# Splitting the weights of attention's query, key and value in the slots of the weight ring

## The chip, the cores and the metric

The kernel runs on one core of a Trainium2 chip. The metric is the device time of one launch in microseconds (us). The kernel before takes 1962.6 us, the median of 3 runs (1962.38 to 1964.43).

## The reference, cut to what matters

One step of a two-layer encoder for 288 tokens (256 of a prompt and 32 of a sample) of width 1024. In each layer one projection feeds all branches of the token mixer:

```python
qa, ka, va, qi, ki, wi, qkv_b, a_b, b_b, z_b, gates = jnp.split(h @ w_in, SPLIT_POINTS, axis=-1)
o_a = dsa_attention(qa, qi, wi, k_all, v_all, ik_all, P)      # indexer scores, top-k keys, softmax over them
c, conv_new = causal_conv(qkv_b, conv_buf, conv_w)            # 1536 channels, then a gated delta rule
y = (g_a * (o_a @ w_oa) + g_b * (o_b @ w_ob)) @ w_out
```

`qa` (the attention's query) has 512 columns, `ka` and `va` (its key and value) 128 each, `qi` (the indexer's query) 512. The indexer computes `relu(qi . ik)`, weighs it by head, masks it and keeps the best keys of each token; the attention runs over these alone. Layer 0 ends in a dense feed-forward part, layer 1 in one of 8 experts, which is most of the span.

## The kernel before, in words

Everything lies transposed: the hidden state `hT` is 8 blocks of 128 channels by 288 tokens. A product of a 128-column weight block with it is one **output**: 8 contraction steps summed in one PSUM bank. A fp32 product is two matmul instructions. Other weights are **split**: ScalarE rounds the block to fp32r (the *high* part), VectorE subtracts it from the original (the *low* part), and three fp32r products (high by high, high by low, low by high) replace the fp32 one. The hidden state is split once a layer too (`hPh` by ScalarE, `hPl` by VectorE in 5 pieces, counted by `hpl_ready`).

**The ring.** All weights come through one ring of 6 slots of 1 MB (`RING`, `SLOT`, 2048 columns of fp32). A *unit* is what one slot holds; unit n lies in slot n modulo 6. SyncE loads the units in order (`load_units`, L339): unit n waits until the counter `unit_used` is at least n - 5, that is, until unit n - 6 has been released. TensorE releases a unit with the first ring matmul that follows its last reading (`rel.due`). An empty `unit()` reserves a slot and loads nothing: a pair of units holds one split block, of which the high part goes into the empty unit's slot and the low part over the weights themselves (`pair_slots`, L417; `ringr` is the same memory as `ring`, typed fp32r).

**The units of a layer**, in `project_units`: 0 small ones (indexer key, decay), 1 and 2 the indexer query, 3 and 4 the attention query (each 4 of 8 contraction blocks by 512 columns, 8 transfers of 128 KB), 5 key and value, and from 6 on 8 pairs for the conv channels and `z` (`pair_unit(l, j)` is 6 + 2j), then the gates.

**The stage around the change** is `front(l)`. Each engine has its own program, in an order written by hand, and waits on counters:

- TensorE: the small product; indexer queries 0 to 3 (`wide`); the decay sums; `indexer(0)`; `wide(P_QA)` (query 0); `indexer(1)`; query 1; `indexer_sample`; query 2; `score_sample`; query 3; key and value (`narrow`); conv 0 (`conv_product`, which uses pair j // 2 and waits for its low part by `pl_ready`); transposes; conv 1, 2, 3; `logits(0, 0)`; conv 4; `logits(0, 2)`; conv 5; and so on. Output m needs the bank of output m - 3 evicted (`room`).
- ScalarE: evictions, relus of the indexer's products, and the high parts of the pairs (`pair_high`, which waits for the weights and for the empty slot). In order: `relus(0)`, eviction of query 0, `relus(1)`, eviction of query 1, `relus_sample`, **`pair_high(0)`**, evictions of query 2, query 3 and key, `pair_high(1)`, eviction of the value, of conv 0, `news`, `pair_high(2)`.
- VectorE: small copies, the low parts of the hidden state, the decays (`g_ready`), a wait for `decay_done`, then `choose(0)`, **`pair_low(0)`**, a copy of the sample's score, `choose(1)`, `pair_low(1)`, `choose(2)`, `pair_low(2)`, and maxima, convolutions and further low parts in turn. `choose(i)` is the top-k of a block of tokens: 8 accumulations (L1430) and some 8 rounds of `max` and `match_replace` (L1438, L1439).
- GpSimd: masks, distances and slopes for the attention (`pen_ready`), then it waits for pair 1.

Of the kernel before, what the change touches and what calls it, by code (L numbers as in the profile page):

```python
# [19 lines left out]
P = 128  # L20
# [53 lines left out]
def program(nc, A, OUT, upto=99):  # L74
    ctx = ExitStack()
    with ctx:
# [169 lines left out]
        def project_units(l):  # L246
# [19 lines left out]
            assert (n0 + 1) % RING < RING - 1 and (n0 + 3) % RING < RING - 1  # L266
# [46 lines left out]
        N_PROJ, N_GATE, N_MERGE, N_FFN, N_EXP = 22, 16, 8, 3 * D_FF // 256, 3 * D_FFE // 256  # L313
# [98 lines left out]
        def pair_unit(l, j):  # L412
            return first["project", l] + 6 + 2 * j

        def pair_slots(l, j):

            n = pair_unit(l, j)  # L417
            return [ring[:, (n % RING) * SLOT:(n % RING) * SLOT + SLOT]] + [
                ringr[:, (x % RING) * SLOT:(x % RING) * SLOT + SLOT] for x in (n + 1, n)]

# [67 lines left out]
        const_ready, ln_turned = sem("const_ready"), sem("ln_turned")  # L488
        lnrow = arena[0:80, 0:P]
        with nc.Block() as block:  # L490
# [24 lines left out]
            def _(pe):  # L515
                pe.wait_ge(const_ready, 1)
                pe.wait_ge(ln_in, 160)
                nc.tensor.transpose(ps[0][:, 0:80], lnrow, ident[0:80, 0:80]).then_inc(ln_turned, 1)

            @block.vector  # L520
            def _(dve):
                dve.wait_ge(ln_turned, 1)
# [5 lines left out]
        masks_ready = sem("masks_ready")  # L528

        def masks(pool):  # L530
# [52 lines left out]
            nc.gpsimd.memset(std[:], 1.0).then_inc(masks_ready, 1)  # L583
# [5 lines left out]
        nrm_turned, out_stored = sem("nrm_turned"), sem("out_stored")  # L589

        def norm(call, j, g_vec=None, b_vec=None, final=False):

            gb = gb_all
            with nc.Block() as block:  # L594
# [15 lines left out]
                def _(dve):  # L610
# [25 lines left out]
                    for k in range(1, 0 if final else KD, 2):  # L636
                        dve.wait_ge(nrm_turned, k + 1)
# [5 lines left out]
                def _(act):  # L643
                    act.wait_ge(var_ready, call + 1)
                    nc.scalar.activation(std[:], rstd[:], ACT.Sqrt).then_inc(std_ready, 1)
                    for k in range(0, 0 if final else KD, 2):
                        act.wait_ge(nrm_turned, k + 1)
# [168 lines left out]
        def front(l):  # L816
# [25 lines left out]
            with nc.Block() as block:  # L842
# [22 lines left out]
                def _(pool):  # L865
# [17 lines left out]
                    nc.gpsimd.tensor_tensor(distr[:], distr[:].bitcast(F32), away[:].bitcast(F32), ALU.subtract).then_inc(pen_ready, 1)  # L883
                    pool.wait_ge(g_ready, l + 1)
# [7 lines left out]
                def _(pe):  # L892
                    def pairview(n):
                        s = (n % RING) * SLOT
                        return ring[:, s:s + 2 * SLOT].rearrange("p (k c) -> p k c", c=512)

# [4 lines left out]
                    def wide(m, n, c):  # L901

                        room(m)
                        w = pairview(n)
                        for k in range(KD):
                            if c == 0 and k % 4 == 0:
# [1909 lines left out]
```

## Time and profile before

| | |
|---|---|
| time, median of 3 runs | 1962.6 us |
| profiled execution | 1963.32 us, of which the span is 1961.5 us |
| TensorE (PE) busy | 1910.4 us |
| VectorE (DVE) busy | 1423.7 us |
| ScalarE (ACT) busy | 1134.7 us |
| GpSimd (POOL) busy | 90.0 us |
| mean granted TensorE clock | 0.991 of full speed |

A row of a timeline gives start and length in us, engine, source line, operation, what it writes and reads with shapes, and in brackets how long the engine sat idle before it and what ended that. Line 359 is the helper through which ring matmuls go; a matmul's length overlaps the next one's, so a group is timed from its start to the start of what follows. PEclk is the granted TensorE clock, 1.00 being 2.4 GHz.

### The profile page before, as it was taken

How to read it: one execution, taken by the hardware profiler on the slowest of the kernel's cores; microseconds unless marked ns; L12 is line 12 of the kernel's file. 1: busy time of each engine (PE TensorE's matmuls, PEld its weight loads, DVE VectorE, ACT ScalarE, POOL GpSimd, SP SyncE). 2: the span in 40 equal slices, each digit the busy share in tenths (PEclk: the TensorE clock that was granted, in tenths of full speed). 3: DMA queues.
4: the chain of work that ended last, by engine and by line, in shares of the span. 5: the costliest groups of instructions: out<-in, count | busy, mean ns of one | idle time of the engine just before them, and what ended most of it. 6: DMA issues, size and time to landing. Idle time of an engine off the chain costs nothing. (4 is left out here: it accounts for less than half of the span.)

```text
span 1961.5 us, 27193 instructions
## 1 busy us (share of the span) xinstructions
PE 1910.4 (97%) x11117; PEld 1649.6 (84%) x11117; DVE 1423.7 (73%) x1600; ACT 1134.7 (58%) x1256; POOL 90.0 (5%) x156
## 2 busy tenths in 40 slices
PE   6999999999999999999999999999999999999995
PEld 5889999999977889998888888888888888888884
DVE  4876265644338763575988979879799798897996
ACT  2465343544334663435776767767677677676773
POOL 5002000100031020001000000000000000000000
PEclk9999999999999999998999999999999999999998
DMA  6232174554421332462999999989999999999992
GB/s 170 86 94 93 44 199 134 172 169 156 153 77 45 93 114 65 104 230 65 372 357 318 370 327 350 370 300 373 344 334 368 318 358 357 317 373 331 343 369 106
DMA packets 260485, 456.98 MB, mean 233 GB/s; under 512 B 32218, under 2 KB 111274, under 8 KB 260356
## 3 DMA queue, kind: packets, MB, share of 16 engines
q1 hardware_dynamic: 258966, 454.74, 67.7%
q8 instruction: 91, 1.49, 0.3%
q10 hardware_dynamic: 1390, 0.44, 0.1%
q14 instruction: 38, 0.31, 0.0%
HBM read 452.11 MB, written 3.04 MB: 232 GB/s over the span
## 5 line engine op out<-in xcount | busy, mean ns | idle before, releaser
L390 DVE TENSOR_TENSOR wl<-ring,wh 128x2048 fp32r<-128x2048 f32 x385 | 880.5, 2289 | 245.3 <-ACT wh L384 242.1
L384 ACT ACTIVATE wh<-ring 128x2048 fp32r<-128x2048 f32 x385 | 739.6, 1923 | 318.0 <-PE ps L359 317.9
L359 PE MATMUL ps<-wh,xgh 128*128 128x512 f32 x896 | 354.3, 395 | 2.4 <-DVE wl L390 2.4
L359 PE MATMUL ps<-wh,xgl 128*128 128x512 f32 x896 | 349.3, 390 | 0.0
L359 PE MATMUL ps<-wl,xgh 128*128 128x512 f32 x896 | 349.1, 390 | 0.0
L359 PE MATMUL ps<-hPh,ringr 128*128 128x288 f32 x1024 | 229.3, 305 | 0.0
L359 PEld LDWEIGHTS ps<-wh,xgh 128*128 128x128 f32 x896 | 168.3, 188 | 40.0 <-DVE wl L390 5.7
L359 PEld LDWEIGHTS ps<-wh,xgl 128*128 128x128 f32 x896 | 168.2, 188 | 35.8
L359 PEld LDWEIGHTS ps<-wl,xgh 128*128 128x128 f32 x896 | 168.4, 188 | 33.2
L359 PEld LDWEIGHTS ps<-hPh,ringr 128*128 128x128 f32 x1024 | 170.6, 189 | 6.2 <-issue 2.5
L359 PE MATMUL ps<-hPl,ringr 128*128 128x288 f32 x512 | 152.0, 297 | 0.0
L359 PE MATMUL ps<-wh,gEh 128*128 128x512 f32 x448 | 143.4, 401 | 0.0
L359 PE MATMUL ps<-wl,gEh 128*128 128x512 f32 x448 | 139.6, 393 | 0.0
L359 PE MATMUL ps<-wh,gEl 128*128 128x512 f32 x448 | 138.1, 389 | 0.0
L359 PE MATMUL ps<-hTh,wh 128*128 128x288 f32 x352 | 103.3, 296 | 0.4 <-ACT hTh L711 0.4
L359 PE MATMUL ps<-hTh,wl 128*128 128x288 f32 x352 | 102.6, 294 | 0.0
L359 PEld LDWEIGHTS ps<-wh,gEl 128*128 128x128 f32 x448 | 84.1, 188 | 19.3
L359 PE MATMUL ps<-hTl,wh 128*128 128x288 f32 x352 | 99.6, 296 | 0.6 <-DVE hTl L2301 0.6
L359 PEld LDWEIGHTS ps<-wl,gEh 128*128 128x128 f32 x448 | 84.0, 188 | 18.9
L359 PEld LDWEIGHTS ps<-hPl,ringr 128*128 128x128 f32 x512 | 97.1, 190 | 0.1
L359 PE MATMUL ps<-hT,ring 128*128 128x288 f32 (+1 forms) x352 | 89.2, 410 | 1.9 <-PEq L594 0.9
L359 PEld LDWEIGHTS ps<-wh,gEh 128*128 128x128 f32 x448 | 78.9, 189 | 12.1
(415 smaller groups left out, 2792.2 us busy)
## 6 DMA issues: line engine op xcount, KB each, us to landing
ring<-in_moe_w SPq DMA_DIRECT2D x336, 1024.0 KB, 5.4
ring<-in_w_in SPq DMA_DIRECT2D x38, 1024.0 KB, 5.2
ring<-in_ffn_w SPq DMA_DIRECT2D x33, 1024.0 KB, 5.2
ring<-in_w_out SPq DMA_DIRECT2D x8, 1024.0 KB, 10.0
ring<-in_w_in SPq DMA_DIRECT2D x32, 128.0 KB, 3.2
ring<-in_w_oa SPq DMA_DIRECT2D x16, 256.0 KB, 5.3
ring<-in_w_ob SPq DMA_DIRECT2D x8, 512.0 KB, 7.2
resid<-in_x_prompt SPq DMA_DIRECT2D x1, 1024.0 KB, 5.2
```

The source lines that it names most:

```text
L359: ins = nc.tensor.matmul(*a, **k)
L384: nc.scalar.activation(wh[:, k % WS, :], ring[:, s:s + SLOT], ACT.Copy).then_inc(hi_ready, 1)
L390: ins = nc.vector.tensor_tensor(wl[:, k % WS, :], ring[:, s:s + SLOT], wh[:, k % WS, :].bitcast(F32), ALU.subtract)
```

## The change

The two query halves and the key/value block are split in ring slots like the conv pairs. Each of these three units is followed by an empty one, so a layer's projection has 25 units and not 22, and conv pair 0 is unit 9 of the layer. ScalarE makes the three high parts (`query_high`), VectorE the low parts of the two query halves, between `g_ready` and its wait for `decay_done`, and GpSimd the low part of key and value, behind `pen_ready`. The six outputs become three fp32r products a step (`query_product`, `query_terms`). The slots of a block are released by two: the first query half and its high part in the middle of query 3 (c == 3, k == 3), the second behind query 3, key/value behind the value. The rest of the orders stays. Besides, some counters are merged: `ln_turned` into `nrm_turned`, `masks_ready` into `const_ready`, `dl_in` into `st_in`.

```diff
@@ project_units
                 unit(*[(v[:, q, :, a, :], w[:, k + q, O_QA + 256 * a:O_QA + 256 * a + 256]
                         .rearrange("p (c x) -> p c x", x=HD)) for q in range(4) for a in range(2)])
+                unit()
             n = len(units)
             unit((slot(n, (8, 256)), w[:, :, O_KA:O_KA + 256]))
+            unit()
...
-        N_PROJ, N_GATE, N_MERGE, N_FFN, N_EXP = 22, 16, 8, 3 * D_FF // 256, 3 * D_FFE // 256
+        N_PROJ, N_GATE, N_MERGE, N_FFN, N_EXP = 25, 16, 8, 3 * D_FF // 256, 3 * D_FFE // 256
...
         def pair_unit(l, j):
-            return first["project", l] + 6 + 2 * j
+            return first["project", l] + 9 + 2 * j
...
+        def query_unit(l, j):
+            return first["project", l] + 3 + 2 * j
+
+        def query_high(act, l, j):
+
+            n = query_unit(l, j)
+            have(act, n)
+            if n + 2 > RING:
+                act.wait_ge(unit_used, n + 2 - RING)
+            w, h, _ = unit_pair(n)
+            nc.scalar.activation(h, w, ACT.Copy).then_inc(qa_high, 1)
+
+        def query_low(eng, engine, l, j, done):
+
+            eng.wait_ge(qa_high, 3 * l + j + 1)
+            w, h, r = unit_pair(query_unit(l, j))
+            engine.tensor_tensor(r, w, h.bitcast(F32), ALU.subtract).then_inc(done, 1)
...
@@ front, GpSimd
                     nc.gpsimd.tensor_tensor(distr[:], distr[:].bitcast(F32), away[:].bitcast(F32), ALU.subtract).then_inc(pen_ready, 1)
+                    query_low(pool, nc.gpsimd, l, 2, ka_low)
                     pool.wait_ge(g_ready, l + 1)
@@ front, TensorE
-                    def narrow(m, n, c):
+                    def query_product(m, c):
 
                         room(m)
                         if c == 0:
-                            have(pe, n)
-                        w = slot(n, (8, 256))
+                            pe.wait_ge(hpl_ready, 5 * (l + 1))
+                        if c == 4:
+                            pe.wait_ge(ka_low, l + 1)
                         for k in range(KD):
-                            ins = rel.mm(ps[m % 3][:, 0:T], w[:, k, P * c:P * c + P], hT[:, k, :], start=(k == 0), stop=(k == KD - 1))
+                            if c == 0 and k % 4 == 0:
+                                pe.wait_ge(qa_low, 2 * l + k // 4 + 1)
+                            for z, (x, y) in enumerate(query_terms(l, k, c)):
+                                ins = rel.mm(ps[m % 3][:, 0:T], x, y, start=(k == 0 and z == 0), stop=(k == KD - 1 and z == 2))
+                            if c == 3 and k == 3:
+                                rel.due, rel.slots = unit_used, 2
                         ins.then_inc(pj_done, 1)
-                        if c == 1:
-                            rel.due = unit_used
+                        if c in (3, 5):
+                            rel.due, rel.slots = unit_used, 2
...
-                    wide(P_QA, u0 + 3, 0)
+                    query_product(P_QA, 0)
                     indexer(1)
-                    wide(P_QA + 1, u0 + 3, 1)
+                    query_product(P_QA + 1, 1)
...
-                    narrow(P_KA, u0 + 5, 0)
-                    narrow(P_VA, u0 + 5, 1)
+                    query_product(P_KA, 4)
+                    query_product(P_VA, 5)
@@ front, ScalarE
                     nc.scalar.activation(hPh[:], hT[:], ACT.Copy).then_inc(hph_ready, 1)
+                    query_high(act, l, 0)
                     evac(P_QI + 1)
...
                     evac(P_QI + 2)
+                    query_high(act, l, 1)
                     evac(P_QI + 3)
                     relus(0)
+                    query_high(act, l, 2)
                     evac(P_QA)
@@ front, VectorE
                     nc.vector.tensor_copy(gvm[0:DEC, 2, 0:H4], gv[0:DEC, 2, :]).then_inc(g_ready, 1)
+                    query_low(dve, nc.vector, l, 0, qa_low)
+                    query_low(dve, nc.vector, l, 1, qa_low)
                     dve.wait_ge(decay_done, l + 1)
```

## Rows read from the trace of the kernel before

**Rows 1.** The page, busy time of each engine and its share of the span.

```profile
PE 1910.4 (97%) x11117; PEld 1649.6 (84%) x11117; DVE 1423.7 (73%) x1600; ACT 1134.7 (58%) x1256; POOL 90.0 (5%) x156
```

**Rows 2.** Busy time by stretch, layer 0: length; PE PEld DVE ACT POOL; clock; DMA.

```profile
47.00:74.50 27.50, 27.50 (x121) 20.03 (x120) 25.89 (x64) 10.11 (x21) 4.16 (x2) 1.00 0.25 77
...
91.30:163.00 71.70, 70.39 (x515) 62.28 (x514) 48.66 (x105) 42.05 (x98) 1.24 (x3) 1.00 0.31 96
```

**Rows 3.** Timeline of TensorE, layer 0: from query 0 to conv 4.

```profile
47.07 4.15 PE L359 MATMUL ps<-hT,ring 128*128 128x288 f32 x16
51.15 2.00 PE L964 MATMUL ps<-arena 64*128 64x256 f32 x16
...
57.15 0.76 PE L975 MATMUL ps<-arena 64*128 64x288 f32 x4
...
61.92 1.16 PE L982 MATMUL ps<-arena 128*32 128x288 f32 x4
63.01 11.91 PE L359 MATMUL ps<-hT,ring 128*128 128x288 f32 x48
...
91.31 0.30 PE L359 MATMUL ps<-hPh,ringr 128*128 128x288 f32 x1
...
94.61 0.70 PE L998 MATMUL ps<-arena 64*128 64x256 f32 x4
```

**Rows 4.** Timeline of VectorE, layer 0: around the three top-k blocks.

```profile
45.25 0.30 DVE L1410 COPY dsm<-ps 128x8 f32<-128x8 f32 x3 [4.31 <-PE ps L1100]
...
46.94 0.35 DVE L1428 TENSOR_SCALAR arena<-arena 128x256 f32<-128x256 f32 x1 [0.90 <-ACT arena L1224]
...
61.14 2.28 DVE L441 TENSOR_TENSOR ringr<-ring,ringr 128x2048 fp32r<-128x2048 f32 x1
...
76.26 2.28 DVE L441 TENSOR_TENSOR ringr<-ring,ringr 128x2048 fp32r<-128x2048 f32 x1
...
87.92 2.27 DVE L441 TENSOR_TENSOR ringr<-ring,ringr 128x2048 fp32r<-128x2048 f32 x1
```

**Rows 5.** Timeline of SyncE's queue, layer 0: the loads of conv pairs 1 and 3.

```profile
47.91 0.37 SPq L347 DMA_DIRECT2D ring<-in_w_in  x1
...
82.67 0.37 SPq L347 DMA_DIRECT2D ring<-in_w_in  x1
```

**Rows 6.** Timeline of ScalarE, layer 0: two evictions, and pair 3's high part.

```profile
35.73 0.39 ACT L1195 ACTIVATE arena<-ps 128x256 f32<-128x256 f32 x1 [2.65 <-PE ps L359]
...
43.49 0.38 ACT L1195 ACTIVATE arena<-ps 128x256 f32<-128x256 f32 x1 [3.41 <-PE ps L359]
...
87.62 1.92 ACT L427 ACTIVATE ringr<-ring 128x2048 fp32r<-128x2048 f32 x1 [1.44 <-DMA ring<-in_w_in]
```

**Rows 7.** One source line, 48.9 to 49.4 us: least, median, longest ns.

```profile
L1430 DVE SCALAR_TENSOR_TENSOR arena<-arena x2: 485/1302/2119, 48.9 to 49.4; 128x256 f32<-128x256 f32 x2
```

**Rows 8.** Timeline of GpSimd, layer 0: its last operation before `pen_ready`.

```profile
49.23 2.02 POOL L883 TENSOR_TENSOR distr<-distr,away 128x864 fp32r<-128x864 f32 x1
```

**Rows 9.** Timeline of TensorE, layer 1: query 3, key and value.

```profile
616.36 11.91 PE L359 MATMUL ps<-hT,ring 128*128 128x288 f32 x48
```

**Rows 10.** Timeline of VectorE, layer 1: low parts of pairs 0 and 2.

```profile
613.84 2.29 DVE L441 TENSOR_TENSOR ringr<-ring,ringr 128x2048 fp32r<-128x2048 f32 x1 [0.89 <-ACT ringr L427]
616.47 0.45 DVE L1493 COPY arena<-ps 32x288 f32<-32x288 f32 x1 [0.34 <-PE ps L982]
...
641.05 2.27 DVE L441 TENSOR_TENSOR ringr<-ring,ringr 128x2048 fp32r<-128x2048 f32 x1
```

**Rows 11.** Busy time by stretch where the granted clock fell.

```profile
251.00:252.00 1.00, 1.00 (x5) 1.00 (x6) 0.99 (x2) 0.00 (x0) 0.00 (x0) 0.50 0.00 0
...
280.00:282.00 2.00, 1.11 (x5) 1.12 (x6) 1.22 (x5) 0.43 (x1) 0.00 (x0) 0.77 1.11 315
```

**Rows 12.** Timeline of TensorE: 12 split products in the delta stage, and what follows.

```profile
250.84 0.61 PE L359 MATMUL ps<-hPh,ringr 128*128 128x288 f32 x1
...
253.84 1.06 PE L1765 MATMUL ps<-arena 128*128 128x128 f32 x8
```

More of the change, by code:

```diff
@@ L265, in project_units @@
                 unit()
-            assert (n0 + 1) % RING < RING - 1 and (n0 + 3) % RING < RING - 1
             return n0
@@ L412, in pair_unit, with unit_pair, query_terms @@
         def pair_unit(l, j):
-            return first["project", l] + 6 + 2 * j
+            return first["project", l] + 9 + 2 * j
         def pair_slots(l, j):
-            n = pair_unit(l, j)
+            return unit_pair(pair_unit(l, j))
+        def unit_pair(n):
             return [ring[:, (n % RING) * SLOT:(n % RING) * SLOT + SLOT]] + [
                 ringr[:, (x % RING) * SLOT:(x % RING) * SLOT + SLOT] for x in (n + 1, n)]
+        qa_high, qa_low, ka_low = sem("qa_high"), sem("qa_low"), sem("ka_low")
+        def query_unit(l, j):
[11 more added lines that the diff above has]
+            engine.tensor_tensor(r, w, h.bitcast(F32), ALU.subtract).then_inc(done, 1)
+        def query_terms(l, k, c):
+            if c < 4:
+                _, h, r = [x.rearrange("p (a b) -> p a b", a=4)[:, k % 4, P * c:P * c + P] for x in unit_pair(query_unit(l, k // 4))]
+            else:
+                _, h, r = [x.rearrange("p (a b) -> p a b", a=KD)[:, k, P * (c - 4):P * (c - 4) + P] for x in unit_pair(query_unit(l, 2))]
+            return (h, hPh[:, k, :]), (h, hPl[k]), (r, hPh[:, k, :])
         def pair_high(act, l, j):
@@ L487, in program @@
         x_in, ln_in = sem("x_in"), sem("ln_in")
-        const_ready, ln_turned = sem("const_ready"), sem("ln_turned")
+        const_ready, nrm_turned = sem("const_ready"), sem("nrm_turned")
         lnrow = arena[0:80, 0:P]
@@ L517, in _ @@
                 pe.wait_ge(ln_in, 160)
-                nc.tensor.transpose(ps[0][:, 0:80], lnrow, ident[0:80, 0:80]).then_inc(ln_turned, 1)
+                nc.tensor.transpose(ps[0][:, 0:80], lnrow, ident[0:80, 0:80]).then_inc(nrm_turned, 1)
             @block.vector
             def _(dve):
-                dve.wait_ge(ln_turned, 1)
+                dve.wait_ge(nrm_turned, 1)
                 dve.wait_ge(x_in, 32)
@@ L526, in _ @@
                 keep(c, "dve")
-        masks_ready = sem("masks_ready")
         def masks(pool):
@@ L582, in masks @@
             c.link(nc.gpsimd.tensor_copy(iota[:], itmp[:, 0:CAP]))
-            nc.gpsimd.memset(std[:], 1.0).then_inc(masks_ready, 1)
+            nc.gpsimd.memset(std[:], 1.0).then_inc(const_ready, 1)
             keep(c, "pool")
@@ L903, in wide @@
                         room(m)
-                        w = pairview(n)
                         for k in range(KD):
+                            w = slot(n + k // 4, (4, 512))
                             if c == 0 and k % 4 == 0:
                                 have(pe, n + k // 4)
-                            ins = rel.mm(ps[m % 3][:, 0:T], w[:, k, P * c:P * c + P], hT[:, k, :], start=(k == 0), stop=(k == KD - 1))
+                            ins = rel.mm(ps[m % 3][:, 0:T], w[:, k % 4, P * c:P * c + P], hT[:, k, :], start=(k == 0), stop=(k == KD - 1))
                             if c == 3 and k == 3:
@@ L1401, in _ @@
                     if l == 0:
-                        dve.wait_ge(masks_ready, 1)
+                        dve.wait_ge(const_ready, 2)
                     c(nc.vector.memset(nrm16, 1.0))
@@ L1544, in program @@
         AC = [r for r in PREP if r not in BY_DVE]
-        dl_in, st_in = sem("dl_in"), sem("st_in")
+        st_in = sem("st_in")
         prep_done, prep_dve, prep_act = sem("prep_done"), sem("prep_dve"), sem("prep_act")
@@ L1750, in decayed @@
                         if q == 0:
-                            pe.wait_ge(st_in, 16 * (l + 1))
+                            pe.wait_ge(st_in, 32 * (l + 1))
                             need("u", 0)
@@ L2140, in _ @@
                     nc.vector.memset(mv[:, 0, 0:1], 1.0).then_inc(unit_used, 1)
-                    dve.wait_ge(dl_in, 16 * (l + 1))
+                    dve.wait_ge(st_in, 32 * (l + 1))
                     for k, i in enumerate((1, 2, 0)):
```

18 lines of the change are left out of this document (6 added, 12 removed).

## The prediction, made before the change was run

> **What bounds the kernel now.** I read the page first: TensorE is busy 97% of the span, so a cheaper product looks like a straight gain [rows 1]. An average over the whole program says nothing about one stage, so the second view is the busy time by stretch. From 47 to 74.5 us (layer 0's attention products, the stage that is changed) TensorE works without a gap, and VectorE is busy for 25.9 of 27.5 us as well; from 91.3 to 163 us TensorE still works 70.4 of 71.7 us and VectorE only 48.7 [rows 2]. So two chains run side by side up to about 91 us and TensorE alone bounds what follows. Which of the two binds at their meeting point is read from the timelines of the two engines.
>
> On TensorE the order is: query product 0, indexer, query 1, sample indexer, query 2, sample score, query 3, key, value, conv 0 to 3, logits, conv 4 at 91.31 [rows 3]. On VectorE: the first top-k (`choose(0)`, from 46.94), the low part of conv pair 0 at 61.14, one copy, `choose(1)`, the low part of pair 1 at 76.26, `choose(2)`, the low part of pair 2 at 87.92, which ends at 90.19 [rows 4]. Conv 4 needs pair 2 and starts at 91.31: VectorE has 1.1 us of slack there and idles nowhere between 46.94 and 90.19. **TensorE is the bound by 1.1 us only**, and whatever it saves before 91 us beyond that is lost. So I ask what the change does to VectorE's chain, and above all to its first link, the low part of pair 0.
>
> **Part 1: the products.** Six outputs per layer (query 0 to 3, key, value) go from 8 fp32 products to 24 fp32r ones. A fp32 output takes 51.15 - 47.07 = 4.08 us from start to next start; a split one, conv 4, takes 94.61 - 91.31 = 3.30 us [rows 3]. Saved: 0.78 us an output, 4.7 us a layer, 9.4 us in both, all of it ahead of conv 4. As 1.1 us is all that VectorE allows, this alone could give 2.2 us.
>
> **Part 2: the high and low halves.** Each query high half on ScalarE costs 1.92 us (the row of a conv pair's) [rows 6]. The first stands behind the copy of the hidden state, in the idle time of 2.65 us that ended at 35.73; the second in the one of 3.41 us that ended at 43.49. Both fit, at nothing. The third follows the first relus, while query 0 still runs, and holds only its eviction, for which nobody waits. The two low parts on VectorE last 2.28 us each, 4.56 us from 40.94, where VectorE idled 4.31 us until 45.25. They overrun by about 0.25 us, ahead of another wait of 0.90 us for the relus at 46.94 [rows 4]. Cost nothing; without the second cover 0.25 us. From below no gain is possible, since nothing is taken from this stretch.
>
> **Part 3: the low part on GpSimd.** The only row near it is its 128x864 subtraction, 2.02 us; by elements 2048 make 4.8 us (estimate; bounds 2.0 and 9.6, twice that) [rows 8]. It runs from about 51.3 in layer 0 and the key product needs it at about 64, so it is covered even at 9.6 us. But it also touches VectorE: beside the 2.02 us subtraction one of VectorE's accumulations (485 ns alone) took 2119 ns; it stood still until GpSimd was done [rows 7, 8]. The new one begins while `choose(0)` still accumulates, so one accumulation will stand for some 4.3 us: `choose(0)` ends near 65.5 and not 61.2. The Trainium skill (SBUF — State Buffer, section "SBUF: two separate sides") says the same of any VectorE operation with two SBUF inputs: the port pair shared with GpSimd is locked for the whole instruction. What that does here, should nothing else be later, is the second rival.
>
> **Part 4: the ring, which decides.** The ring has 6 slots. Before, units 0 to 5 of a layer (small, 2 for the indexer, 2 for the query, key/value) filled it, and conv pair 0 was unit 6, loaded as soon as unit 0 was used, 25 us ahead of its need. Now each query half takes two slots and so does key/value, so pair 0 is unit 9. Its loading waits for `unit_used` at 4: for slot 3, where the *low part of the first query half* lies, which is read last in the middle of query product 3. The orders on ScalarE and VectorE around it are unchanged: ScalarE makes pair 0's high half between the sample relus and the eviction of query 2, and VectorE makes its low part between `choose(0)` and `choose(1)`. Both will stand at it. Step by step, from rows 3:
> - query 0: 47.07 + 3.30 = 50.37; indexer 1.93 (its 2.00 less the 0.07 by which such a group overlaps the next: 61.92 + 1.16 against 63.01): 52.30; query 1: 55.60; sample indexer 0.69 (0.76 less 0.07): 56.29; query 2: 59.59; sample score 1.09 (61.92 to 63.01): 60.68; half of query 3: 62.33.
> - release to issue: a unit freed by query 0's first product (47.07) had its successor issued at 47.91 [rows 5]; 0.84 us less 0.38, as an fp32r product is that much shorter: issue at 62.8.
> - issue to high half: pair 3's load was issued at 82.67 and ScalarE began at 87.62, 4.95 us [rows 5, 6]: 67.75. High half 1.92: low part starts at 69.7.
>
> Before it started at 61.14, so VectorE's chain is **8.5 us later** (and the 4.3 us of part 3 vanish in this wait). From there to pair 2's low part it is unbroken [rows 4]: 87.92 + 8.5 = 96.45, done at 98.7. TensorE meanwhile: key ends at 67.3, value waits for query 2's eviction behind the high half until 70.1 and ends at 73.4, conv 0 at 76.7, the transposes and conv 1 at 81.1, then **6 us of idle** until pair 1's low part (76.26 + 8.5 + 2.28 = 87.0), conv 2 and 3 and the first logits (2.5 us) until 96.1, idle again, conv 4 at 98.75 against 91.31: **+7.4 us** in layer 0.
>
> Layer 1 is the same stage 553.35 us later (63.01 and 616.36) [rows 3, 9]. There the low part of pair 0 started at 613.84 and would now at 69.7 + 553.35 = 623.05: +9.2. A wait of 0.34 us behind it is absorbed. Pair 2's low part: 641.05 + 8.9 = 649.95, done at 652.2; conv 4 stood at 91.31 + 553.35 = 644.66: **+7.5 us** [rows 10].
>
> Does it come back? After conv 4 TensorE idled 1.3 of 71.7 us [rows 2], and all its releases move with it: no. The other edits (semaphores merged) cost nothing: each wait's other condition is met tens of us before. Sum 7.4 + 7.5 = 14.9. The profiled execution took 1963.32 us, 0.7 over the median of 1962.6 that I add it to: **1977.6 us**.
>
> **The clock** is what these rows don't fix. The granted clock fell (a mean of 0.77) in two us in which TensorE idled for 0.9, and in the delta stage stood at its lower level of 1.2 GHz (0.50) with no idle at all, behind matmuls of few rows [rows 11]. There 12 split products took 3.00 us (250.84 to 253.84), not half of 3.30: 1.35 us lost [rows 12]. New idle times of 3, 6 and 2.6 us could each bring that. Those before conv 4 are covered (VectorE decides until 98.75, 2.6 us after TensorE is ready); one behind it costs up to 1.35 us a layer. I take 0, the warm end, since the last idle is the shortest, and keep 1.35. The Trainium skill (TensorE: Matmul & The Clock Gate, "HAM oscillation — how this bites in real kernels") says that gaps in which the array waits for data put it back to half clock; by it the 6 us idle would do so surely, and conv 2 would run cold, within that cover.
>
> **Rivals.**
> - *The ring doesn't bind and TensorE's saving arrives*: all 9.4 us, 1953.2. For it: TensorE is 97% busy. Against: VectorE's slack of 1.1 us, and the load's place, which is arithmetic on the ring. 4%.
> - *GpSimd's subtraction is what holds VectorE*, and pair 0's load lands in time. VectorE is 4.3 us later in layer 0, conv 4 at 94.5 (+3.2); in layer 1 `choose(0)` ends at 617.3 against the old low part's 613.84, conv 4 +1.8: 1967.6. It decides if pair 0's high half is done before 65.5. 6%.
> - *The clock or the load makes it worse*: conv 4 begins cold in both layers (+2.7: 1980.3), or conv 2 and 3 run cold throughout (48 products at 0.25 us, 12.0 us, and TensorE itself reaches conv 4 at 101.5: +2.8 a layer, 1983.1). 11%.
> - *Part of the delay returns* after conv 4, or the change nearly evens out (1958.7 to 1966.5): 3%.
> - The forecast: 76%; its own range is 1974 to 1980 (a landing 1 us earlier or later in each layer, and a us of chain).
>
> The range to hold 8 in 10 is 1971 to 1983: it leaves out the first two rivals and the worst of the third. A measurement of this kernel can tell 0.2%, 3.9 us. Faster by more: 0.04; within: 0.03; slower: 0.93.
>
> **What the changed profile would show.** The load of pair 0 issued near 62.8 us; ScalarE's high half with a wait for a DMA until about 67.7; VectorE idle for 4 to 8 us after `choose(0)`, low part at 69.7; one VectorE accumulation of over 4 us; TensorE idle for 3 us before the value product and for 6 us before conv 2; conv 4 at 98.7 and at 652.2; the six outputs at 3.3 us each. A pair 0 load issued before 58 us, or VectorE going straight from `choose(0)` to the low part, would prove me wrong; so would a conv 4 at or before 91.3.

## The result, and the profile after

The changed kernel takes 1980.47 us (median of 4 runs, 1980.33 to 1982.01) against 1963.51 us of the one before (4 runs, 1962.38 to 1964.83): a ratio of 1.0088 [1.0070, 1.0105], 17.0 us slower. The forecast was 1977.6: 14.9 us more than the 1962.6 us that the kernel before had in three runs (its terms are rounded). The profiled execution took 1982.01 us, its span is 1979.7 us.

The page still shows a TensorE that looks like the bound: its busy share fell by one point only, from 97% to 96%.

```profile
PE 1909.9 (96%) x11213; PEld 1658.9 (84%) x11213; DVE 1435.9 (73%) x1604; ACT 1145.3 (58%) x1262; POOL 104.0 (5%) x158
```

**Where the time arises.** ScalarE loads an activation table at fixed places of the program. Two of them frame what is called the front stage of a layer below: one stands ahead of the attention products, one at the start of the delta rule; a third ends the next stretch. The first block has these rows of the kernel before (timeline of ScalarE: start, length, line), the second the same of the changed kernel.

```profile
36.22 1.28 ACT L1288 ACT_TABLE_LOAD   x1
161.57 1.28 ACT L1833 ACT_TABLE_LOAD   x1 [0.55 <-PEq L842]
271.32 1.28 ACT L1900 ACT_TABLE_LOAD   x1
589.57 1.28 ACT L1288 ACT_TABLE_LOAD   x1
714.74 1.28 ACT L1833 ACT_TABLE_LOAD   x1 [0.27 <-PEq L842]
```

```profile
36.65 1.28 ACT L1321 ACT_TABLE_LOAD   x1
170.56 1.28 ACT L1870 ACT_TABLE_LOAD   x1 [0.27 <-PEq L873]
280.63 1.28 ACT L1937 ACT_TABLE_LOAD   x1
598.92 1.28 ACT L1321 ACT_TABLE_LOAD   x1
732.55 1.28 ACT L1870 ACT_TABLE_LOAD   x1 [0.27 <-PEq L873]
```

Layer 0's front stage went from 125.35 to 133.91 us (+8.56), layer 1's from 125.17 to 133.63 (+8.46): 17.02 together, as much as the medians differ. From 271.32 to 589.57 us the old kernel takes 318.25 us and the new one 318.29; the stretch behind layer 1's front stage, to the next table load, 108.49 and 108.51 us. Layer 0's delta rule, from the end of its front stage to the next table load, took 109.75 us before and 110.07 now. Nothing is given back. (At the first row the new trace is also 0.43 us later; that is taken off below.)

**The chain in layer 0 and in layer 1**, by the timelines of SyncE's queue (SPq), ScalarE, VectorE and TensorE. L459 is the high part of a conv pair, L473 its low part, L1479 the end of a top-k, L360 the ring matmuls. The first ten rows are layer 0, the rest layer 1; `x2` in the first row are the loads of pair 0 (63.41) and pair 1 (65.02):

```profile
63.41 1.97 SPq L348 DMA_DIRECT2D ring<-in_w_in  x2
68.58 1.91 ACT L459 ACTIVATE ringr<-ring 128x2048 fp32r<-128x2048 f32 x1 [10.89 <-DMA ring<-in_w_in]
60.43 0.85 DVE L1479 TENSOR_SCALAR away<-arena 128x256 fp32r<-128x256 f32 x1
70.52 2.29 DVE L473 TENSOR_TENSOR ringr<-ring,ringr 128x2048 fp32r<-128x2048 f32 x1 [9.24 <-ACT ringr L459]
70.90 0.40 PE L360 MATMUL ps<-hPh,ringr 128*128 128x288 f32 x1 [2.89 <-ACT arena L1232]
88.08 0.58 PE L360 MATMUL ps<-hPh,ringr 128*128 128x288 f32 x1 [6.16 <-DVE ringr L473]
97.31 2.27 DVE L473 TENSOR_TENSOR ringr<-ring,ringr 128x2048 fp32r<-128x2048 f32 x1
99.72 0.37 PE L360 MATMUL ps<-hPh,ringr 128*128 128x288 f32 x1
105.89 1.92 ACT L459 ACTIVATE ringr<-ring 128x2048 fp32r<-128x2048 f32 x1 [2.21 <-DMA ring<-in_w_in]
109.68 1.09 PE L1058 MATMUL ps<-ident,arena 128*128 128x128 f32 x8 [0.70 <-ACT arena L1270]
...
625.69 0.38 SPq L348 DMA_DIRECT2D ring<-in_w_in  x1
631.22 1.91 ACT L459 ACTIVATE ringr<-ring 128x2048 fp32r<-128x2048 f32 x1 [11.25 <-DMA ring<-in_w_in]
633.16 2.29 DVE L473 TENSOR_TENSOR ringr<-ring,ringr 128x2048 fp32r<-128x2048 f32 x1 [6.66 <-ACT ringr L459]
650.72 0.58 PE L360 MATMUL ps<-hPh,ringr 128*128 128x288 f32 x1 [3.48 <-DVE ringr L473]
659.94 2.27 DVE L473 TENSOR_TENSOR ringr<-ring,ringr 128x2048 fp32r<-128x2048 f32 x1
662.41 0.32 PE L360 MATMUL ps<-hPh,ringr 128*128 128x288 f32 x1
```

Almost the whole forecast can be seen in these rows. Pair 0's load is issued at 63.41 us, ScalarE stands 10.89 us for it, VectorE is through with its first top-k at 61.28 and stands 9.24 us for the high part. The low part of pair 0 starts at 70.52, where it started at 61.14 [rows 4]. TensorE waits twice ahead of conv 4, which starts at 99.72 where it started at 91.31 [rows 3]. A third wait, 2.6 us just before conv 4, was forecast too, and it isn't there: TensorE works through to 99.72, and pair 2's low part ends at 97.31 + 2.27 = 99.58.

**The granted clock** in some stretches of the new kernel (the columns are those of [rows 2]):

```profile
88.00:93.00 5.00, 4.92 (x20) 4.95 (x21) 4.66 (x16) 0.00 (x0) 2.39 (x3) 0.50 0.63 198
96.00:99.00 3.00, 3.00 (x22) 2.04 (x20) 2.90 (x6) 1.96 (x4) 0.00 (x0) 1.00 0.01 3
633.00:639.00 6.00, 5.46 (x23) 5.46 (x24) 5.63 (x9) 3.01 (x8) 0.00 (x0) 0.50 0.02 6
```

Behind the idle times, TensorE ran at 1.2 GHz (0.50): conv 2 in both layers (in layer 1 from 650 to 656 us), and the value product in layer 1. Ahead of conv 4 in layer 0 it was at 2.4 GHz again (1.00). Conv 2, conv 3 and the first logits were put at 9.1 us and took 11.6 (88.08 to 99.72), which is where the third wait went.

**GpSimd and VectorE.** The timeline row of GpSimd's low part in layer 0 (L443):

```profile
56.54 4.59 POOL L443 TENSOR_TENSOR ringr<-ring,ringr 128x2048 fp32r<-128x2048 f32 x1
```

And two single lines, VectorE's accumulations and GpSimd's small operations on the slopes (count; least, median and longest ns):

```profile
L1467 DVE SCALAR_TENSOR_TENSOR arena<-arena x28: 483/485/4677, 47.8 to 639.2; 128x256 f32<-128x256 f32 x28
L908 POOL TENSOR_SCALAR slopes<-ident x16: 277/278/4567, 40.0 to 593.3; 32x32 fp32r<-32x32 f32 x16
```

### The profile page after: what moved, and what is told of

The parts are those of the page before. It is cut to its first block and busy times, and to the rows that moved or that the text cites. A ratio compares the mean times of both kernels' runs of the same rounds, so it can differ in the third digit from the quotient of the medians.

```text
span 1979.7 us, 27407 instructions
## 1 busy us (share of the span) xinstructions
PE 1909.9 (96%) x11213; PEld 1658.9 (84%) x11213; DVE 1435.9 (73%) x1604; ACT 1145.3 (58%) x1262; POOL 104.0 (5%) x158
## 5 line engine op out<-in xcount | busy, mean ns | idle before, releaser
L360 PE MATMUL ps<-wh,xgh 128*128 128x512 f32 x896 | 354.5, 396 | 2.1 <-DVE wl L391 2.1
L360 PE MATMUL ps<-wh,xgl 128*128 128x512 f32 x896 | 349.4, 390 | 0.0
L360 PE MATMUL ps<-wl,xgh 128*128 128x512 f32 x896 | 349.0, 390 | 0.0
L360 PE MATMUL ps<-hPh,ringr 128*128 128x288 f32 x1216 | 276.4, 310 | 15.8 <-DVE ringr L473 9.6
L360 PEld LDWEIGHTS ps<-hPh,ringr 128*128 128x128 f32 x1216 | 207.5, 194 | 25.8 <-issue 14.9
L360 PEld LDWEIGHTS ps<-wh,xgh 128*128 128x128 f32 x896 | 168.3, 188 | 39.7 <-DVE wl L391 5.5
L360 PEld LDWEIGHTS ps<-wh,xgl 128*128 128x128 f32 x896 | 168.2, 188 | 36.0
L360 PEld LDWEIGHTS ps<-wl,xgh 128*128 128x128 f32 x896 | 168.4, 188 | 33.2
L360 PE MATMUL ps<-hPl,ringr 128*128 128x288 f32 x608 | 183.4, 302 | 0.0
L360 PE MATMUL ps<-wh,gEh 128*128 128x512 f32 x448 | 143.4, 401 | 0.0
L360 PE MATMUL ps<-wl,gEh 128*128 128x512 f32 x448 | 139.6, 393 | 0.0
L360 PE MATMUL ps<-wh,gEl 128*128 128x512 f32 x448 | 138.1, 389 | 0.0
L360 PEld LDWEIGHTS ps<-hPl,ringr 128*128 128x128 f32 x608 | 118.3, 195 | 0.0
L360 PE MATMUL ps<-hTh,wh 128*128 128x288 f32 x352 | 103.3, 296 | 0.4 <-ACT hTh L742 0.4
L360 PE MATMUL ps<-hTh,wl 128*128 128x288 f32 x352 | 102.6, 294 | 0.0
L360 PEld LDWEIGHTS ps<-wh,gEl 128*128 128x128 f32 x448 | 84.1, 188 | 19.4
L360 PE MATMUL ps<-hTl,wh 128*128 128x288 f32 x352 | 99.6, 296 | 0.6 <-DVE hTl L2338 0.6
L360 PEld LDWEIGHTS ps<-wl,gEh 128*128 128x128 f32 x448 | 84.0, 188 | 18.8
L360 PEld LDWEIGHTS ps<-wh,gEh 128*128 128x128 f32 x448 | 78.9, 189 | 12.0
L459 ACT ACTIVATE ringr<-ring 128x2048 fp32r<-128x2048 f32 x32 | 61.1, 1910 | 44.1 <-DMA ring<-in_w_in 44.1
```

The lines of the kernel that those rows point to most:

```text
L360: ins = nc.tensor.matmul(*a, **k)
L459: nc.scalar.activation(h, w, ACT.Copy).then_inc(ph_ready, 1)
```

## The experiments

All runs in one table: median and number of runs, the ratio to the kernel before on the same chip, and by how much each front stage of the profiled execution is longer than in the kernel before (from the same table loads as above). The kernel before had a median of 1962.46 us beside e1 to e4, 1963.47 beside e5 to e8, 1963.04 beside e9 and e10 and 1961.95 beside e11; the recorded ratio is not exactly the quotient of the medians. The code shown is drawn together from the edits, and `...` marks lines left out.

| run | us | ratio [95%] | layer 0 | layer 1 |
|---|---|---|---|---|
| after | 1980.47 (4) | 1.0088 [1.0070, 1.0105] | +8.56 | +8.46 |
| e1 ring alone | 1986.29 (4) | 1.0116 [1.0100, 1.0133] | +11.52 | +11.13 |
| e2 first wait moved | 1966.62 (9) | 1.0025 [1.0015, 1.0035] | -0.50 | +2.72 |
| e3 key/value alone | 1972.78 (4) | 1.0056 [1.0039, 1.0073] | +4.38 | +2.60 |
| e4 query alone | 1969.99 (5) | 1.0041 [1.0027, 1.0055] | +2.88 | +3.06 |
| e5 no low part on GpSimd | 1978.77 (4) | 1.0084 [1.0069, 1.0099] | +8.33 | +8.66 |
| e6 TensorE kept busy | 1981.45 (4) | 1.0092 [1.0077, 1.0108] | +9.16 | +9.31 |
| e7 whole new order | 1962.16 (11) | 0.9998 [0.9989, 1.0007] | -1.67 | -1.72 |
| e8 e7 and e5 | 1961.87 (11) | 0.9995 [0.9986, 1.0004] | -1.89 | -0.08 |
| e9 new order, no splits | 1964.06 (11) | 1.0007 [0.9998, 1.0016] | +1.05 | +0.46 |
| e10 earlier release | 1959.88 (11) | 0.9983 [0.9974, 0.9992] | -3.27 | -0.85 |
| e11 e10, layer 1 mended | 1959.80 (11) | 0.9986 [0.9977, 0.9995] | -3.46 | -0.98 |

**e1: the ring's part alone.** The units, slots and releases of the change, but fp32 products and no high or low parts of query, key and value.

```diff
-query_high(act, l, 0..2); query_low(dve, ..., 0), (dve, ..., 1), (pool, ..., 2)
-for z, (x, y) in enumerate(query_terms(l, k, c)):
-    ins = rel.mm(..., x, y, ...)
+ins = rel.mm(ps[m % 3][:, 0:T], x, hT[:, k, :], start=(k == 0), stop=(k == KD - 1))
```

> The changed kernel with its ring (25 units a layer, the three empty ones, pair 0 as unit 9, the same releases), but the query, key and value products in fp32 again and no high or low part of them on any engine. Theory of the ring: pair 0 is still loaded only in the middle of query 3, and that now comes 2.7 us later, since the fp32 outputs take 4.08 us. By the rows of before: issue at 65.7 us, low part of pair 0 near 72.8 against 61.14, conv 4 10.5 us later than before, in layer 1 10.7: 1984 to 1986 us, slower than the changed kernel (1980.5). Rival, that the new splitting work, GpSimd's subtraction above all, is what costs: with all of it gone the time is that of before, 1963.5 us.

Measured 1986.29, 0.3 us above the expected 1984 to 1986. VectorE stands for the high part (timeline), as in the whole change and longer, since the slower products release the slot later:

```profile
72.86 2.29 DVE L473 TENSOR_TENSOR ringr<-ring,ringr 128x2048 fp32r<-128x2048 f32 x1 [12.16 <-ACT ringr L459]
102.05 0.37 PE L360 MATMUL ps<-hPh,ringr 128*128 128x288 f32 x1 [0.88 <-DVE ringr L473]
```

The ring's slots by themselves cost 23.8 us (1986.29 - 1962.46; 22.65 in the two front stages), more than the whole change. The split products give some 6 of that back, by an earlier release: in layer 0 pair 0's load is issued 29.55 us after the first table load in e1, and 26.76 us after it in the changed kernel. That is part 4 of the prediction, shown.

**e2: the same ring, another order around the wait.** ScalarE evicts query 2, 3 and key ahead of pair 0's high part; VectorE copies the scores and begins the second top-k, and makes pair 0's low part ahead of its fifth round.

```diff
-pair_low(dve, l, 0)
 dve.wait_ge(sum_done, l + 1)
 nc.vector.tensor_copy(score2[0:DEC, :], ps[6][0:DEC, 0:SMAX]).then_inc(sum_read, 1)
-choose(1)
+choose(1, {4: lambda: pair_low(dve, l, 0)})
```

> The changed kernel with the two halves of the wait moved and nothing else: ScalarE makes pair 0's high part behind the evictions of query 2, query 3 and key, and VectorE makes its low part inside the second top-k, ahead of its fifth round (at about 70 us), with the copy of the sample's score ahead of that top-k. The load is issued as late as in the changed kernel. Theory: what hurts is not the late load but that VectorE's chain stands at it; that wait of 9.2 us (layer 0) and 6.7 us (layer 1) goes. VectorE's chain then ends pair 2's low part near 90.4 us in layer 0 (conv 4 0.9 us earlier than before) and, as GpSimd's subtraction holds an accumulation for 4.7 us there, 1.6 us later than before in layer 1: 1963 to 1966 us. Rival, that the late load itself costs TensorE the time: little moves, above 1975 us.

Measured 1966.62, 0.6 us above the expected range. The load comes no earlier (26.79 us after the table load, 26.76 in the changed kernel), yet of the 17.0 us only 4.2 are left (timelines of VectorE and TensorE):

```profile
70.38 2.29 DVE L473 TENSOR_TENSOR ringr<-ring,ringr 128x2048 fp32r<-128x2048 f32 x1 [0.37 <-ACT ringr L459]
626.72 0.58 PE L360 MATMUL ps<-hPh,ringr 128*128 128x288 f32 x1 [4.13 <-DVE ringr L473]
```

So the harm is not the late load but what is queued behind it: the second top-k on VectorE and three evictions on ScalarE. Both were moved at once, and no run says which of the two counts for how much. In layer 1 something is left: TensorE waits 4.13 us before conv 0, since VectorE comes late by itself (see e10), and then runs at 0.50 until 632 us. The profiled execution was the fastest of the nine (1964.07 us); the 2.5 us up to the median lie in executions that have no trace.

**e3 and e4: one half of the change each.** e3 splits key and value alone (one more unit: pair 0 is unit 7), e4 the query alone (two more: unit 8).

```diff
-N_PROJ = 25; pair_unit: first["project", l] + 9 + 2 * j
+e3: N_PROJ = 23; pair_unit: ... + 7 + 2 * j; query by wide(), no high or low parts of it
+e4: N_PROJ = 24; pair_unit: ... + 8 + 2 * j; key and value with hT, no high or low parts of them
```

> Only key and value are split (the query products are fp32, in one slot each; 23 units a layer, pair 0 is unit 7, loaded in the middle of the indexer's last query output, near 42 us). The ring does not bind, and what is left of the cost is GpSimd's subtraction beside the first top-k. Second rival of the prediction: one accumulation of VectorE stands 4.3 us in each layer, conv 4 3.2 and 1.8 us later than before: 1968.5 us. If that lock costs nothing: 1.1 us a layer gained at most, 1961.3 us. Ring theory says only that it is well below the changed kernel.

> Only the query is split (key and value fp32 in one slot; 24 units a layer, pair 0 is unit 8 and its high part lies in unit 9's slot). The load is in time (unit used by 47.9 us), but the empty slot is that of the first query half, free in the middle of query 3: ScalarE starts the high part at 62.8 and not at 67.8. Theory of the ring: low part of pair 0 at 64.8, conv 4 2.5 us later than before in layer 0 and 2.7 in layer 1: 1968.7 us (1966 to 1971). Nothing is subtracted on GpSimd, so the theory of the lock says no loss: 1963.5 or below.

Measured 1972.78 and 1969.99: e4 as expected, e3 4.3 us over. In e4 pair 0's load had landed long before, and ScalarE stood for the empty slot alone (timeline); conv 4 comes 2.86 and 2.84 us later than before, where 2.5 and 2.7 were expected. As nothing is subtracted on GpSimd there, this loss is the ring's:

```profile
65.24 1.92 ACT L458 ACTIVATE ringr<-ring 128x2048 fp32r<-128x2048 f32 x1 [5.74 <-PE ps L359]
```

e3's rows, by timeline:

```profile
51.10 5.16 DVE L1461 SCALAR_TENSOR_TENSOR arena<-arena 128x256 f32<-128x256 f32 x2
94.04 0.37 PE L359 MATMUL ps<-hPh,ringr 128*128 128x288 f32 x1 [2.41 <-DVE ringr L472]
```

and by stretch, just behind conv 4:

```profile
95.00:98.00 3.00, 3.00 (x16) 3.00 (x15) 2.08 (x7) 1.46 (x8) 0.00 (x0) 0.54 0.78 236
```

Here pair 0's load comes in time, and what delays VectorE is that it stands still beside GpSimd's subtraction, the lock of the prediction's part 3: two accumulations took 5.16 us beside GpSimd's low part, 0.97 alone, and VectorE went on to the low part of pair 0 at 64.83 without a wait: conv 4 comes 58.34 us after the first table load, not 55.09 (+3.25; the second rival had +3.2), and in layer 1 +1.51 (it had +1.8). The rest of its front stages, 1.1 us each, lies behind the start of conv 4, before which TensorE waited 2.41 us and then ran at 0.54 (in layer 1 2.41 us too): this is the clock's cost *on* the path, priced at up to 1.35. Of the four runs two took 1969.8 and 1969.9 us and two 1975.7; the profile is that of a faster one. What lies between them is told under the hardware.

**e5: the low part of key and value moved from GpSimd to VectorE**, behind the first top-k.

```diff
 choose(0)
+query_low(dve, nc.vector, l, 2, ka_low)
```

> The changed kernel with one step moved: the low part of key and value is subtracted by VectorE behind the first top-k, where it idled 9.2 us (layer 0) and 6.7 us (layer 1), and not by GpSimd. The accumulation that stood 4.7 us in layer 1 then takes 0.49. Theory of the ring: both changes lie inside VectorE's wait for pair 0, so the time stays that of the changed kernel, 1979 to 1982 us. Theory of the lock (GpSimd's subtraction holds VectorE and that is what costs): 4 to 8 us less, 1972 to 1976.

Measured 1978.77, 0.2 us under the expected 1979 to 1982 and far from the 1972 to 1976 of the lock: the ring's theory holds. The longest accumulation is 530 ns and not 4677 (the single line), and VectorE still stands (timeline):

```profile
L1466 DVE SCALAR_TENSOR_TENSOR arena<-arena x28: 483/485/530, 47.6 to 637.6; 128x256 f32<-128x256 f32 x28
```

```profile
70.23 2.29 DVE L473 TENSOR_TENSOR ringr<-ring,ringr 128x2048 fp32r<-128x2048 f32 x1 [7.46 <-ACT ringr L459]
```

**e6: TensorE kept busy** with 3 idle products before the value and 6 before conv 2, so that its clock stays up.

```diff
+pe.wait_ge(decay_read, l + 1); idle_products(3)
 query_product(P_VA, 5)
...
+pe.wait_ge(new_evac, 3 * (l + 1)); idle_products(6)
 conv_product(2)
```

> The changed kernel with idle matmuls (fp32, 512 columns, about 0.9 us each) in TensorE's two waits: 3 ahead of the value output, 6 ahead of conv 2. Nothing else waits less. If the clock's fall to half behind these waits costs, then the value output of layer 1 and conv 2 of both layers run at full clock, TensorE reaches conv 4 up to 2 us earlier, and conv 4 is bound by pair 2's low part again as the prediction had it (98.75 us): 0.5 us gained in layer 0, 1 in layer 1, 1978 to 1980 us. If the clock is no part of the cost: 1980.5 or, as the idle matmuls can overrun a wait, up to 1 us more.

Measured 1981.45, no gain in the median. But the four runs lie in two pairs, 1978.7 and 1978.8 us (mean granted clock 0.992 both) and 1984.1 and 1984.3 (0.989 and 0.988), and the profile is that of the slowest. In it conv 2 ran at full clock now (88 to 93 us at 1.00, not 0.50), and TensorE waited before conv 4. By stretch and by timeline:

```profile
88.00:93.00 5.00, 5.00 (x40) 5.00 (x39) 4.66 (x16) 0.57 (x3) 1.83 (x3) 1.00 0.67 210
99.00:102.00 3.00, 2.93 (x13) 2.96 (x14) 2.89 (x7) 1.93 (x8) 0.00 (x0) 0.54 0.45 127
```

```profile
99.07 0.41 PE L360 MATMUL ps<-hPh,ringr 128*128 128x288 f32 x1 [2.41 <-DVE ringr L473]
```

Conv 4 comes 63.09 us after the table load, in the changed kernel 63.07 (99.72 - 36.65); in layer 1, where it waited 2.39 us, 63.06 against 63.49. So the cold stretches of the changed kernel lie in VectorE's shadow, but for some 0.2 us in layer 1 at most (662.41 against a low part done at 662.21). With them gone, an idle time of 2.4 us stood just before conv 4, and the slow clock behind it, on the path: in this execution the front stages are 0.6 and 0.85 us longer than in the changed kernel. The faster pair lies 1.5 us below every run of the changed kernel and inside the expected 1978 to 1980; that the clock did not fall behind conv 4's wait in it would fit its mean clock, but it has no trace. What keeping TensorE busy is worth stays open.

**e7 and e8: the whole order fitted to the late loads.** The low parts of pairs 0 and 1 inside the second top-k, that of pair 2 ahead of the third, first maxima and first convolution inside the third; ScalarE's order is that of e2. e8 has e5's edit as well.

```diff
-pair_low(dve, l, 0); ...; choose(1); pair_low(dve, l, 1); choose(2); pair_low(dve, l, 2); maxima(0, 0, 2); conv(0)
+choose(1, {2: lambda: pair_low(dve, l, 0), 5: lambda: pair_low(dve, l, 1)})
+pair_low(dve, l, 2)
+choose(2, {7: between})      # between: maxima(0, 0, 2); conv(0)
```

> The moved order taken further, from what the timelines show: pair 0's and pair 1's low parts inside the second top-k (ahead of its third and sixth round), pair 2's low part ahead of the third top-k, whose result is not needed before the sample's logits, and the first maxima and convolution inside that top-k ahead of its eighth round. VectorE's chain is then no longer the bound, and TensorE keeps what the split saves less its wait for pair 0 (to about 72.6 us): conv 4 near 89.4 us in layer 0 against 91.31, as much in layer 1: 1957.5 to 1960 us, faster than before. If the ring's late load cannot be got round by order, not below 1963.

> The same order, and the low part of key and value on VectorE behind the first top-k. VectorE has 2.2 us more to do ahead of pair 0's low part and no accumulation that stands 4.7 us in layer 1; both end near the moment at which pair 0's high part is ready. Equal to the previous kernel within 1 us: 1957.5 to 1960.5 us. If GpSimd's subtraction costs something in that one, this is up to 2 us faster.

Measured 1962.16 and 1961.87, 2.2 and 1.4 us above the expected ranges: the loss is gone, the hoped-for gain isn't there (0.9998 and 0.9995, both intervals hold 1). TensorE still waits before conv 0, so that of the 4.7 us a layer that the products were to save 1.7 arrive (timeline of e7):

```profile
71.82 0.37 PE L360 MATMUL ps<-hPh,ringr 128*128 128x288 f32 x1 [1.73 <-DVE ringr L473]
92.49 0.70 PE L1030 MATMUL ps<-arena 64*128 64x256 f32 x4 [0.65 <-ACT arena L1270]
624.24 0.37 PE L360 MATMUL ps<-hPh,ringr 128*128 128x288 f32 x1 [2.17 <-DVE ringr L473]
```

In layer 1 of e8 hardly anything arrived (-0.08 us, against -1.72 in e7), though TensorE waited equally long before conv 0, 2.14 us and 2.17. The clock differs, by stretch from the start of conv 0, first e8, then e7:

```profile
623.97:627.00 3.03, 3.03 (x13) 3.03 (x14) 2.82 (x10) 0.63 (x2) 0.00 (x0) 0.50 0.39 110
624.24:627.24 3.00, 3.00 (x23) 3.00 (x23) 2.79 (x10) 0.28 (x1) 0.00 (x0) 1.00 0.47 136
```

The two front stages differ by 1.64 us, about what a fall of the clock costs elsewhere (1.3 to 1.6 us, below), so whether e8's edit brings anything can't be read from them. Both kernels have the merged counters of the change as well, and reach the old time with them: the counters carry no part of the 17 us that can be seen.

**e9: that order in the kernel before, without the splits.**

> The kernel before with the order of e7 on VectorE (low part of pair 1 inside the second top-k, low part of pair 2 ahead of the third, the first maxima and conv 0 inside the third), without the three splits. Theory: in the kernel before TensorE has not one gap from 47 to 101 us, so an order that frees VectorE earlier brings nothing by itself: 1961.5 to 1965, and the 1.5 to 1.7 us that e7's profile won in each front stage come from the cheaper products. Rival: they come from the order; then this one wins as much without the splits, and lies at 1958.5 to 1961.

Measured 1964.06 (1.0007), inside the expected 1961.5 to 1965. Conv 4 comes 55.10 us after the table load (90.99 - 35.89), before 55.09. The order alone brings nothing at conv 4, so what e7 wins there (52.95) comes from the products. Behind conv 4 the order costs: TensorE waits 0.98 us for the exponentials at 101.15 us, and the front stages are 1.05 and 0.46 us longer. (e10's own order was not run without the splits.)

**e10: the release itself made earlier.** TensorE computes query 3 ahead of the sample indexer, and the sample score behind the key. ScalarE evicts query 2 and 3 ahead of the sample relus, then makes pair 0's high part ahead of the key's eviction.

```diff
-indexer_sample(); query_product(P_QA + 2, 2); score_sample(); query_product(P_QA + 3, 3); query_product(P_KA, 4)
+query_product(P_QA + 2, 2); query_product(P_QA + 3, 3); indexer_sample(); query_product(P_KA, 4); score_sample()
...
+choose(1, {3: first_low, 7: lambda: pair_low(dve, l, 1)})
+choose(2, {2: lambda: pair_low(dve, l, 2), 6: between})
```

> e7 with query 3 moved ahead of the sample indexer and the sample score behind the key product, so that the slot which pair 0's load waits for is released some 1.8 us earlier; the high half of pair 0 ahead of the key's eviction, the low parts of pairs 0, 1 and 2 and the copy of the sample scores inside the top-k rounds. Theory (the ring release is the one thing that holds the front stage, and TensorE's saving arrives when it doesn't): the waits of 1.73 and 2.17 us before conv 0 and that of 0.65 us before the logits go, conv 0 starts near 70.2 us, each front stage is 1.5 to 2.2 us shorter than in e7: 1957 to 1960. Rival: the next link is late at once (pair 1's or pair 2's load, or a top-k end that comes later), TensorE waits for it instead: 1961 to 1964.

Measured 1959.88, 0.9983 [0.9974, 0.9992]: inside the expected 1957 to 1960, and faster than both kernels, by 3.2 us against the one before. (e7's interval reaches down to 0.9989, so the two medians alone don't tell e10 from e7.)

```profile
86.48 0.30 PE L360 MATMUL ps<-hPh,ringr 128*128 128x288 f32 x1
619.13 2.29 DVE L473 TENSOR_TENSOR ringr<-ring,ringr 128x2048 fp32r<-128x2048 f32 x1
621.56 0.37 PE L360 MATMUL ps<-hPh,ringr 128*128 128x288 f32 x1 [2.92 <-DVE ringr L473]
```

In layer 0 TensorE has no wait before conv 4, which comes 51.25 us after the table load: 3.8 us earlier than before. Layer 1 wins only 0.85 us, less than the 1.72 of e7, where 1.5 to 2.2 us more were expected: a miss for that layer. The load is issued there 24.65 us after the table load and not 26.78, but pair 0's low part stands a round later in the top-k and starts 35.06 us after it, in e7 34.31. GpSimd's low part holds an accumulation of VectorE (7.80 us for seven that take 3.61 alone) in both, and with the ring out of the way that shows, as 2.92 us before conv 0.

**e11: pair 0's low part three rounds earlier in layer 1.**

```diff
-choose(1, {3: first_low, ...
+choose(1, {(3, 0)[l]: first_low, ...
```

> e10 with the low part of pair 0 three top-k rounds earlier in layer 1 only. There GpSimd's low part still holds one accumulation of VectorE for some 4.2 us, so in e10 the low part of pair 0 began 2.9 us later than in layer 0 and TensorE waited 2.92 us before conv 0; its high half was done 3.0 us before. Theory: with the ring out of the way VectorE's own lateness from the lock is what is left; the wait of 2.92 us in layer 1 goes, and 2.5 to 2.9 us of the span with it: 1956 to 1958. Rival: layer 1's next link (the top-k end, pair 1's low part) takes the wait over: 1959 to 1961.

Measured 1959.80, where the theory said 1956 to 1958 and the rival 1959 to 1961. The wait before conv 0 shrank to 0.40, and another took over, before conv 2:

```profile
621.52 0.37 PE L360 MATMUL ps<-hPh,ringr 128*128 128x288 f32 x1 [0.40 <-DVE ringr L473]
630.96 0.37 PE L360 MATMUL ps<-hPh,ringr 128*128 128x288 f32 x1 [1.66 <-DVE ringr L473]
```

With a further 0.61 us before the transposes of `turn(0)` the front stage is 0.13 us shorter than in e10: the rival held. Moving one low part forward only moved VectorE's lateness to the next. Whether the 4.2 us that its accumulation stands for GpSimd are what is late would be told by e11 with e5's edit, which was not run.

## Why the prediction was right

**The place of pair 0's load** (part 4): right. Issue 63.41 - 0.43 = 62.98 against 62.8, and e1 shows that the slots alone do it. The 0.2 us come from the outputs ahead of it: query 0 took 3.39 us to the start of the indexer (47.50 to 50.89) and not 3.30, a figure taken from conv 4, and queries 1 and 2 as much.

**From issue to high part**: 4.95 us was taken from a load issued by itself. Here it took 5.17 us (63.41 to 68.58), in layer 1 5.53. Pair 1's load follows 1.6 us behind in both; that it is the reason is not shown, since in the kernel before a load alone in the queue took 5.4 us to land as well (issued at 621.08 us). With 0.2 us at the issue that puts the low part of pair 0 at 70.09 on the old scale (69.7 predicted), and layer 1's 0.8 us later than worked out (34.24 us after the table load, not 33.48).

**The unbroken chain on VectorE**: right. Conv 4 came +7.98 (7.4 predicted) and, counted from 598.92, +8.37 (7.5 predicted; in the kernel before it started at 644.69).

**Nothing returns behind conv 4**: right in sign. In layer 0 0.58 us more was lost, which was not in the prediction: the softmax's exponentials stand on ScalarE behind pair 4's high part, whose load came late as well (the wait of 0.70 us at 109.68). The sum is 7.98 + 0.58 + 8.37 + 0.09 = 17.02 against 14.9.

**TensorE's waits**: 2.89 us before the value (3 predicted), 6.16 before conv 2 (6 predicted); in layer 1 3.25 and 3.48, the second shorter since the value ran cold. The third, 2.6 us before conv 4, was predicted and did not come.

**The clock taken at 0**: right for the path, with some luck. After 6.16 us of idle time conv 2 ran at 0.50. The Trainium skill (TensorE: Matmul & The Clock Gate, "HAM oscillation — how this bites in real kernels") has it that a block of matmuls behind a long wait for data starts cold; the trace agrees. The cover of 2.6 us held, but the cold stretch used up all of it: TensorE was ready for conv 4 together with VectorE in layer 0 and some 0.2 us behind it at most in layer 1. One more cold stretch ahead of conv 4 would have come on top. The price kept in reserve, 1.35 us, was met as 1.1 us in e3, where the wait lay directly before conv 4.

**GpSimd's low part** (part 3): size right, place wrong in layer 0. It took 4.59 us (4.8 estimated) and held one accumulation in layer 1, which lasted 4677 ns. In layer 0 it held none, since it began at 56.54 and not at 51.3: GpSimd had itself stood some 4.3 us for VectorE's two low parts (an operation of 278 ns took 4567). So VectorE was free at 61.28 and idled 9.24 us, where 4 to 8 were expected. Either way it is hidden in the wait for pair 0, as e5 shows, and e3 shows its full price once it isn't.

**The saving of the products**: right that it is lost (1.1 us of slack on VectorE). e7 and e10 show what it takes to get at it.

The mechanism was right, then, and the forecast 2 us too low for three small terms: some 0.5 us in layer 0 and 0.8 in layer 1 from outputs and loads that took longer than the rows they were priced by, and the 0.58 us behind conv 4.

## What to carry to other kernels

Where weights come through a ring, every slot that an edit takes moves all later loads: count which release the next load waits for, before counting what the edit saves. A late load costs what stands behind its first user in each engine's fixed order: putting the evictions and a top-k ahead of that user took away 12.8 of 17.0 us with the load as late as before. A cheaper product pays only as far as the other chain has slack; look at which wait takes over before mending the one in front. Here the whole repair brought 3.2 us of the 9.4 that the cheaper products promise.

## What the runs showed of the hardware

**The lock between GpSimd and VectorE works both ways.** VectorE's accumulation of 485 ns, begun at 613.15 us, stood for GpSimd's subtraction, begun at 612.96 (it took 4677 ns). And a 32x32 operation of GpSimd, 278 ns alone, begun at 41.33, stood for VectorE's two subtractions, begun at 41.28 (4567 ns). The rounds of `max` and `match_replace` ran beside GpSimd's subtraction at their normal length (timeline of the changed kernel):

```profile
59.45 0.43 DVE L1475 MAX8 arena<-arena 128x8 f32<-128x256 f32 x1
```

The single-input operation behind them (60.43, 0.85 us, elsewhere 0.29) ended at 61.28 us, just behind GpSimd's at 61.13. The Trainium skill (SBUF — State Buffer, "Who interferes with whom") has it that the order of issue decides who stands; the trace agrees: in both cases the one that began second stood.

**The clock falls at places that the change doesn't touch, in some executions.** The stretch behind the front stage took 109.75 us in the kernel before, with the clock at 0.50 in part of it [rows 11], and 108.49 us in e2 (161.27 to 269.76), where it stayed at full speed. By stretch, first before, then e2:

```profile
161.00:271.00 110.00, 109.67 (x922) 103.77 (x923) 52.40 (x94) 49.97 (x117) 11.02 (x9) 0.98 0.27 80
```

```profile
161.00:271.00 110.00, 109.69 (x934) 103.95 (x935) 53.89 (x100) 51.51 (x117) 11.03 (x9) 1.00 0.28 80
```

The same came at a second place: 108.49 us from 714.74 to 823.23 before, 110.03 in e6. At a third the clock fell in both, for 10.2 us before and for 6.8 in e2: 25.79 us from 885.39 to 911.18 before, 24.52 in e2. Each is worth 1.3 to 1.6 us. Runs of one kernel spread by several us (1957.1 to 1962.8 in e11), and their time goes with the mean granted clock of the execution, which is on record for each: 0.993 in e11's two fastest, 0.989 to 0.990 in the three above 1961.3; 0.991 in e3's two runs at 1969.8 and 1969.9, 0.989 and 0.987 in the two at 1975.7; and e6's two pairs. So a difference of 2 us needs the front stages' rows as well as the medians. That such falls explain all of the spread is argued and not shown: only one execution of each kernel has a trace.

**Equal waits, unequal clock.** Behind 2.14 us of idle time the clock stood at 0.50 in e8, behind 2.17 us it stayed at 1.00 in e7, at the same place of the program. What decides between the two, no run here shows.
